# One kernel, four edits: logits in the last block, high parts gathered first, ring pieces returned singly, own buffers for the adaLN blocks

## The reference

```
mod = silu(c) @ ada_w + ada_b                    # 1024 x 6144: six vectors of 1024
u   = rms_norm(x) * (1 + scale_a) + shift_a
x   = x + gate_a * mixer(u)                      # w_in: 1024 x 10760, mLSTM and dilated attention,
                                                 # two branch projections, one output projection w_out
u   = rms_norm(x) * (1 + scale_f) + shift_f
x   = x + gate_f * moe(u)                        # 16 experts, top 2 of one group of 4
out = rms_norm(x) * final_norm_g

moe: scores = sigmoid(u @ router_w); two experts a row; weights = scores / their sum
     out += weight * ((silu(u @ w_gate[e]) * (u @ w_up[e])) @ w_down[e])   # 1024x512, 1024x512, 512x1024
```

## Time and profile before

| | |
|---|---|
| median of 3 runs | 637.62 us (637.15 to 639.16) |
| the profiled execution, its own time | 639.07 us |
| its span in the trace | 637.30 us |
| PE busy | 593.4 us, 93% |
| PE weight loads busy | 444.7 us, 70% |
| DVE, ACT busy | 326.7 us (51%), 225.2 us (35%) |
| read from HBM | 183.16 MB, 289 GB/s over the span |

### The profile page before, as it was taken

How to read it: one execution, slowest core, us unless ns; L and a number is a source line. 1 busy time by engine, 2 the same in 40 slices (tenths; PEclk the granted TensorE clock), 3 DMA queues, 4 the chain that set the end, 5 groups by cost and what they waited for, 6 DMA issues and landing times.

```text
span 637.3 us, 8441 instructions
## 1 busy us (share of the span) xinstructions
PE 593.4 (93%) x3581; PEld 444.7 (70%) x3581; DVE 326.7 (51%) x515; ACT 225.2 (35%) x300; POOL 5.6 (1%) x13
## 2 busy tenths in 40 slices
PE   4697999999999999999999999889999999998783
PEld 4697988999998888999999886533543533533231
DVE  3895986775758977787454655302212112120103
ACT  3424658544454365665552443201111111110103
POOL 3000000000000000000000000000000000000000
PEclk9997999999999999999999997799999999999997
DMA  8996454877767867725699699199999999999981
GB/s 314 358 359 229 143 194 133 283 259 242 255 216 264 319 214 261 258 77 195 198 338 344 219 374 388 48 398 387 401 387 402 386 401 387 401 387 401 387 325 67
DMA packets 86313, 184.78 MB, mean 290 GB/s; under 512 B 5401, under 2 KB 5505, under 8 KB 86273
## 3 DMA queue, kind: packets, MB, share of 16 engines
q1 hardware_dynamic: 83746, 184.06, 79.9%
q10 hardware_dynamic: 2528, 0.16, 0.3%
HBM read 183.16 MB, written 1.05 MB: 289 GB/s over the span
## 4 chain that ended last, share of the span: by engine, by line
PE 85%; DMA 8%; DVE 3%; ACT 1%; issue 1%; SPq 1%; DVEq 0%; ACTq 0%
PE ps L1287 32%; PE ps L1295 15%; PE ps L1495 14%; PE ps L1506 7%; DMA ring<-in_w_down_e_dram 3%; PE ps L1485 2%; DMA ring<-in_w_gate_e_dram 2%; DMA ring<-in_w_up_e_dram 2%; PE ps L1529 2%; DMA raw<-in_ada_w_dram 1%; PE ps L1235 1%; PE ps L1358 1%; PE ps L1382 1%; PE ps L1397 1%; PE ps L1244 1%
## 5 line engine op out<-in xcount | busy, mean ns | idle before, releaser
L1287 PE MATMUL ps<-u_hi,hi 128*128 128x256 f32 x448 | 130.8, 292 | 9.3 <-DVE u_lo L815 9.3
L755 DVE TENSOR_TENSOR lo<-raw,hi 128x2048 fp32r<-128x2048 f32 x52 | 118.7, 2289 | 35.6 <-ACT hi L514 35.3
L1287 PE MATMUL ps<-u_lo,hi 128*128 128x256 f32 x448 | 128.7, 287 | 0.0
L1287 PE MATMUL ps<-u_hi,lo 128*128 128x256 f32 x448 | 128.6, 287 | 0.0
L1495 PE MATMUL ps<-ring,xe_t 128*64 128x512 f32 x512 | 113.8, 594 | 7.9 <-DMA ring<-in_w_up_e_dram 4.4
L514 ACT CAST hi<-raw 128x2048 fp32r<-128x2048 f32 x52 | 98.8, 1907 | 50.0 <-PE ps L1287 24.8
L1287 PEld LDWEIGHTS ps<-u_hi,hi 128*128 128x128 f32 x448 | 88.0, 196 | 9.6 <-DVE u_lo L815 9.5
L1495 PEld LDWEIGHTS ps<-ring,xe_t 128*64 128x64 f32 x512 | 37.1, 137 | 76.0 <-issue 75.7
L1287 PEld LDWEIGHTS ps<-u_lo,hi 128*128 128x128 f32 x448 | 88.0, 197 | 0.1
L1287 PEld LDWEIGHTS ps<-u_hi,lo 128*128 128x128 f32 x448 | 87.9, 196 | 0.0
L1506 PE MATMUL ps<-ring,he_t 128*64 128x512 f32 x256 | 57.1, 596 | 1.5 <-DMA ring<-in_w_down_e_dram 0.8
(11 more groups left out here) (276 smaller groups left out, 797.0 us busy)
## 6 DMA issues: line engine op xcount, KB each, us to landing
raw<-in_w_in_dram SPq DMA_DIRECT2D x42, 1024.0 KB, 5.3
ring<-in_w_gate_e_dram SPq DMA_DIRECT2D x32, 1024.0 KB, 14.6
ring<-in_w_up_e_dram SPq DMA_DIRECT2D x32, 1024.0 KB, 14.2
ring<-in_w_down_e_dram SPq DMA_DIRECT2D x32, 1024.0 KB, 14.6
raw<-in_ada_w_dram SPq DMA_DIRECT2D x24, 1024.0 KB, 5.5
raw<-in_w_branch_m_dram SPq DMA_DIRECT2D x4, 1024.0 KB, 5.5
raw<-in_w_out_dram SPq DMA_DIRECT2D x4, 1024.0 KB, 7.5
raw<-in_w_branch_a_dram SPq DMA_DIRECT2D x2, 1024.0 KB, 6.4
```

Source lines behind the costliest of these rows:

```text
L755: V.tensor_tensor(lo[b % RING][:], src[:], hi[b % RING][:].bitcast(F32), ALU.subtract).then_inc(lo_ready, 1)
L1287: ins = mm(dst, w[:, k, cols], x[:, k0 + k, :], start=(first and c % 2 == 0 and k == 0 and n == 0), stop=(end and k == KB - 1 and n == 2), ...
```

## The change

1. **ada blocks.** The eight first ada blocks get buffers of their own (`first_ada`), so that the w blocks 0 to 3 and the ada blocks are all loaded without waits but two. A block is now 256 rows (two a partition) by shift and scale columns together, landed by two transfers of 512 KB. All eight are DVE's, two instructions of 128x(2x512) each. The sixteen later ones are one row a partition by 2048 columns, one DVE instruction each. ACT instead of DVE scales x; two matmuls on x are put ahead of its transposes; block 0 takes its contraction step by step, as quarters of u_lo come.
2. **Last block.** The first half of the logits goes between t=0 and t=1 of the last block, the transposes of x_res for t=0 into its t=1.
3. **Gather.** xg_lo is computed behind the one-hot tables, and the first gather takes all high parts and then all low parts.
4. **Pieces.** `chunk_used` counts pieces, not half groups; each piece is waited for and returned by itself. For that the four matmuls of one expert stand together. A ring slot moves from 120 to 176 KB, and so do xg_hi and result in exchange.

```diff
+        first_ada = [at(f"first_ada{a}", k, [P, 2, 2, NB]) for a, k in enumerate((96, 104, 112, 144, 48, 72, 164, 156))]
...
+            for kind, n in FIRST:
+                if kind == "w":
+                    sp.dma_start(raw[n][:], block_source((kind, n))).then_inc(raw_loaded[n], 16)
+                else:
+                    if n == 6:
+                        after(sp, "x_ss")
+                    if n == 7:
+                        after(sp, "x_t")
+                    j, k = n // KB, 2 * (n % KB)
+                    for i in range(2):
+                        sp.dma_start(first_ada[n][:, i], ada_first[:, k + i, 0:2, j * NB:(j + 1) * NB]
+                                     ).then_inc(ada_landed[n], 16)
...
-            ada(1)
+            for a in range(4):
+                ada(a)
+                if a == 0:
+                    after(dve, "vec_t")
+                    event(V.tensor_copy(vec[:], ps[0][:, 0:104]), "vec")
+            split_lo(0)
+            modulate(0, 1)
+            split_first()
+            split_lo(1)
             ada(4)
             ada(5)
-            modulate(0, 1)
-            split_lo(0)
-            u_split_lo(0)
-            split_lo(1)
-            ada(2)
-            ada(3)
...
+                    for c in range(4):
+                        if s == EARLY - 1 and c == 2:
+                            after(pe, "x_up")
+                            mod_columns(1, 7)
...
+                            if s == NBLK - 1 and t == 1 and k == 1:
+                                after(pe, "x1_1_t0")
+                                for c in range(KB):
+                                    tr_ins = tr(ps[6][:, c * P:(c + 1) * P], x_res[:, 0, NB + c * P:NB + (c + 1) * P], ident[:])
+                                event(tr_ins, "x1_turn1_t0")
                         if s == NBLK - 1 and t == 0:
                             event(ins, "wo_t0")
+                            after(pe, "x1_turned0", "mod3")
+                            logits(0, 0)
+                            logits(1, 0)
...
             def gate_or_up(bank, half, slots, col):
 
-                for k in range(KB):
-                    kk = KB * half + k
-                    for s in range(2):
-                        w = ring[slots[s]][:].rearrange("p (k n) -> p k n", k=KB)
+                for s, slot in enumerate(slots):
+                    w = ring[slot][:].rearrange("p (k n) -> p k n", k=KB)
+                    for k in range(KB):
+                        kk = KB * half + k
                         ins = mm(ps[bank][64 * s:64 * s + 64, :], xe_t[:, kk, col + s * SLOTS:col + (s + 1) * SLOTS], w[:, k, :],
                                  start=(kk == 0), stop=(kk == KT - 1))
-                ins.then_inc(group_used, 1)
+                    ins.then_inc(chunk_used, 1)
...
-            pe.wait_ge(xg_split, TT)
+            after(pe, "xg_hi1")
             pe.wait_ge(onehot_ready, 1)
             for kb in range(4):
-                gather_part(kb, 4 * SLOTS, 4 + kb)
+                gather_part(kb, 4 * SLOTS, 4 + kb, (0,))
+            pe.wait_ge(xg_split, TT)
+            for kb in range(4):
+                gather_part(kb, 4 * SLOTS, 4 + kb, (1,))
```

More of the change, by code:

```diff
@@ L528, in _ @@
             event(A_(st[:, 4:6], st[:, 2:4], ACT.Sqrt), "x_sqrt")
+            after(act, "x_rms")
+            for t in range(TT):
+                ins = A_(x_in[:, t, :], x_in[:, t, :], ACT.Copy, scale=st[:, 6 + t:7 + t])
+            event(ins, "x_norm")
             act.dma_start(w_if[:], A["w_in"][0].rearrange("(k p) n -> p k n", p=P)[:, :, IF_AT:IF_AT + IF_N]).then_inc(small_loaded, 16)
@@ L542, in u_split_hi @@
                 event(ins, f"u_hi{j}")
-            split_hi(0)
-            u_split_hi(0)
+            after(act, "x_up", "chan0")
+            for k in range(KB):
+                event(A_(u_hi[:, k, :], x_t[:, k, :], ACT.Identity, scale=chan[:, 2, k:k + 1], bias=chan[:, 0, k:k + 1]),
+                      f"u_hi0_{k}")
             split_hi(1)
@@ L758, in ada @@
             def ada(a):
+                if a < ADA_FIRST:
+                    j = a // KB
+                    dve.wait_ge(ada_landed[a], 32)
+                    dst = acc_a[:, :, j * NB:(j + 1) * NB]
+                    if a % KB:
+                        dve.wait_ge(ada_done, a)
+                    for i in range(2):
+                        kk = 2 * (a % KB) + i
+                        if kk == 0:
+                            step(V.tensor_scalar(dst, first_ada[a][:, i], cs[:, 0:1], None, ALU.mult))
+                            continue
+                        ins = V.scalar_tensor_tensor(out=dst, in0=first_ada[a][:, i], scalar=cs[:, kk:kk + 1], in1=dst,
+                                                     op0=ALU.mult, op1=ALU.add)
+                        if i == 0:
+                            step(ins)
+                    ins.then_inc(ada_done, 1)
+                    return
@@ L769, in ada @@
[L769 to L779 removed]
+                if k:
+                    dve.wait_ge(ada_done, a)
@@ L810, in modulate, with split_first @@
                 event(ins, f"u_f32_{j}")
+            def split_first():
+                after(dve, "u_f32_0")
+                for k in range(KB):
+                    after(dve, f"u_hi0_{k}")
+                    event(V.tensor_tensor(u_lo[:, k, :], u_f32[:, k, :], u_hi[:, k, :].bitcast(F32), ALU.subtract), f"u_lo0_{k}")
             def u_split_lo(j):
@@ L1100, in _ @@
                                       st[:, 28 + t:29 + t], None, ALU.mult)
-            for t in range(TT):
-                after(dve, f"xg_hi{t}")
-                V.scalar_tensor_tensor(out=xg_lo[:, t, :], in0=x_res[:, t, :], scalar=st[:, 14 + t:15 + t],
-                                       in1=xg_hi[:, t, :].bitcast(F32), op0=ALU.mult, op1=ALU.subtract).then_inc(xg_split, 1)
             after(dve, "rank_sums")
@@ L1156, in _ @@
             build_onehot(0)
+            for t in range(TT):
+                after(dve, f"xg_hi{t}")
+                V.scalar_tensor_tensor(out=xg_lo[:, t, :], in0=x_res[:, t, :], scalar=st[:, 14 + t:15 + t],
+                                       in1=xg_hi[:, t, :].bitcast(F32), op0=ALU.mult, op1=ALU.subtract).then_inc(xg_split, 1)
             event(V.tensor_scalar(many_i[:, 0:1], many[:, 0:1], float(SLOTS), None, ALU.is_gt), "many")
@@ L1256, in _, with logits @@
             event(ins, "x_t")
-            pe.wait_ge(rows_loaded, 80)
-            event(tr(ps[0][:, 0:104], rows[0:104, :], ident[0:104, 0:104]), "vec_t")
-            mod_columns(0, 0, 1)
-            mod_columns(0, 1, 1)
+            mod_columns(0, 1)
+            def logits(t, h):
+                for k in range(KB):
+                    ins = mm(ps[4][:, t * NE:(t + 1) * NE], x_res_t[h][:, k, t * P:(t + 1) * P], rw_scaled[:, KB * h + k, :],
+                             start=(t == 0 and h == 0 and k == 0), stop=(h == 1 and k == KB - 1), skip_group_check=True)
+                return ins
             for s, (g, k0, first, end) in enumerate(BLOCKS):
                 kind, _, channel_major = GROUP_LIST[g]
-                if s == 0:
-                    after(pe, "u_lo0", "x_up")
                 if s == EARLY:
```

232 lines of the change are left out of this document (107 added, 125 removed).

## The result

| | before | after |
|---|---|---|
| median | 638.39 us (637.15 to 639.40, 4 runs) | 655.65 us (654.55 to 656.03, 4 runs) |
| span of the profiled execution | 637.30 us | 653.70 us |
| PE busy | 593.4 us, 93% | 618.6 us, 95% |

The changed kernel is slower: ratio 1.0268, interval 1.0243 to 1.0294. The forecast was 651 us, in a range of 628 to 662.

The account below looks back on a forecast made before the run. In the expert stage PE and DMA are both full, PE only 8.7 us faster. Head -6.0, last block and gather -1.2, expert stage +20.5 make +13.3 us: 650.9 by the median of 637.62, called 651; range 628 to 662.

Parts of the forecast that it names:

- The order of the matmuls: Expert stage: one expert's four matmuls together start the second expert four passes late; +20.5 us net of 8.7 us of waits.
- the DMA share: Expert stage, sign in the profile after: the DMA share would be below 1 after 415 us.
- the estimate of five instructions waiting ahead of a column half: PE's queue in the expert stage: 28 instructions shared, then five before each column half; gives a lag of four passes.
- 17 runs x 1.72: Expert stage: each of 17 runs of half groups pays four passes, 1.72 us, once at its end; 29.2 us in all.
- The head: Start up to block 3, ada blocks and PE's earlier start, with the clock staying up: -6.0 us (1.4 to 9.4).
- The estimate of an ada instruction of 1024: Head, on DVE: one ada instruction of 1024 takes some 1.3 us, 2.6 a block (bounds 0.78 and 1.56).
- Last block and gather: Between the head and the expert stage: net -1.2 us for the stage's start (bounds -3.0 and +0.5).
- The block's share: Last block: logits and transposes moved in delay its end 2.4 us but save one turn; +0.8 us (+2.3 to -1.0).
- the gather's: Gather: xg_lo, 2.48 us, leaves the way of the rank sums; about 2.0 us gained.
- The single returns: Expert stage: returning one piece at a time gains nothing on the first release and nothing at the end.
- PE passing all sixteen instructions: Expert stage rival: the new order costs nothing, DMA stays the bound; -7.2 us, 630.4 us; chance 0.31 with short lags.
- lags of one or two: Expert stage: second expert starting one or two passes late, 7.3 us per pass on PE, would give 630 to 635 us.

Follow-up runs that it names:

- e1: Kernel before with only the loop order changed: one expert's four matmuls stand together ahead of the other's; 661.74 us, ratio 1.0368.
- e3: Changed kernel with the experts taking turns of two matmuls each; 630.80 us, ratio 0.9888.
- e4: Changed kernel with turns of three matmuls of the first expert, three of the second, then one and one; 636.59 us, ratio 0.9977.
- g3: e2 with all eight matmuls of the first expert ahead of the second's eight, in the first pair's gate only; 640.21 us in one run.
- f1: e2 with last block and gather as in the kernel before; 632.94 us, ratio 0.9917.
- e2: Changed kernel with only the turns restored, one matmul of each expert in turn; single waits and releases stay; 630.30 us, ratio 0.9880.
- f2: e2 with the last block alone as in the kernel before, logits behind it; 629.28 us, ratio 0.9864.
- g1: e2 with logits behind the last block (f2) and the last eight pieces loaded in halves (f4); 628.87 us, ratio 0.9857.
- f3: e2 with waits and returns by half group, two pieces at a time; 632.44 us, ratio 0.9898.
- f4: e2 with the last eight pieces each loaded as two transfers of 512 KB; 628.82 us, ratio 0.9856.

## Why the prediction was right

**The order of the matmuls decides: right.** Forecast: a lag of four passes, a gate group of some 8.8 us, no PE wait on ring pieces. Seen: 4 passes begun in the first 1.78 us and 8 in the next 1.72, 8.94 us, no wait. One sign did not come as forecast: the DMA share did not fall below 1 after 415 us but stayed at 1.04 up to 563, and fell only when the loads were all in. The slower PE did not hold the loads up; it fell behind them. e1 shows the cause by itself, 23.6 us; e3, e4 and g3 show the count behind it (0, 2 and 12 passes where the estimate of five instructions waiting ahead of a column half says 0, 2 and 12). The Trainium skill (TensorE: Matmul & The Clock Gate, Part 3, The mechanism) has matmuls in program order in start and end; here the second expert's first pass begins together with the first expert's fifth, at 401.88, and ahead of its last three, so that between the two column halves this does not hold. Its queue of 64 (the table at its start), whose window it gives for weight loads, does not cover it either: eight instructions, passes among them, can be passed without loss, sixteen cannot.

**Its size: some 4 us too small.** I took 17 runs x 1.72 = 29.2 us. A run of two costs 1.85 and a run of four 2.07, so 10 x 1.85 + 7 x 2.07 = 33.0: beside the four passes each change from one half group to the next costs another 0.1 us or so, which four passes of 0.43 leave out; what makes it up was not looked into. 33.0 - 8.7 = 24.3, against 23.35 + 0.4 measured.

**The head: right in sum and parts.** Forecast 6.0; the books give 6.1, f1 5.3 in the times and 5.6 in the trace. The first block at 27.25 (forecast 27.0), block 3's at 49.92 (49.7), the idle stretch ahead of it 1.05 us (about 1), and the clock of 54 to 85 us at 1.00 instead of 0.93. The estimate of an ada instruction of 1024, 1.3 us, held: DVE took 8.03 us for six of them, 1.34 each, and was through with the first four blocks at 20.65 (20.5).

```profile
12.62 8.03 DVE L797 SCALAR_TENSOR_TENSOR acc_a<-first_ada,cs,acc_a 128x1024 f32<-128x1024 f32 x6
```

**Last block and gather: right at the clock of the profiled run.** Forecast -1.2, measured -1.3 in the books, where both kernels ran the larger part of the gather at the lower clock. The block's share was +0.8 and came out as +1.0 by the traces of e2 and f2; the gather's was -2.0 and came out as -2.3 by what is left in the books, and as -2.6 at most between f1 and g1. What the prediction left out is that the clock there changes from run to run and moves the start of the experts by up to 2 us: the 3.7 us between f1 and f2 hold some of it. It held that at full clock 0.6 us of xg_lo would show; f2 ran the gather at full clock, and 0.15 us showed. That the profiled run fell where the working assumed it was luck.

**The single returns: right.** Costed at nothing, and f3 gives 0.1 us.

**The rivals.** PE passing all sixteen instructions would come to the same as turns restored: 7.2 us faster than before. Those measured 638.17 - 630.30 = 7.9 us (6.6 to 8.7 by the interval), so the sum without the order's cost held. That 630.3 stands so close to the forecast 630.4 is partly chance, since the forecast went by 637.62 us for the kernel before and e2 stands beside 638.17. The "630 to 635" for lags of one or two was a slip: by the prediction's own 7.3 us for each pass a lag of two gives 14.6 - 8.7 - 7.2 = -1.3, so 636.3 us, and e4, with that lag, measured 636.6.

**The total.** Forecast +13.3 us, measured +16.4 between the two profiled executions and +17.3 between the medians. Of the 3.1 us between the first two, the order's cost makes 3.3 (23.35 + 0.4 measured, 20.5 forecast), and the head and the middle gained 0.1 each more than forecast. The other 0.9 us lie between profiled executions and medians, and no term of the sum stands for them.

## What to carry to other kernels

Where small matmuls share the array by column halves, let them take turns in the program: here two of one expert in a row were free and four cost 1.85 us at every run of half groups. Before making an engine's order serve a finer hand-over, compare its cost with the slack of that engine (8.7 us here) and with what the finer hand-over can bring (0.1 us). Test such an order on its own: three edits that gained 8 us were hidden behind one that lost 25.

## What was not expected of the hardware

**The clock behind the last block is not the same from run to run.** Up to the first gather matmul the changed kernel, e2, e3, e4, f3 and f4 differ in nothing on PE. Granted clock in 384 to 391 us, when PE has just had gaps of 0.7 us between small matmuls: the changed kernel, at the lower level of 1.2 GHz, then e2, between the two levels.

```profile
384.00:391.00 7.00, 6.62 (x14) 3.89 (x15) 4.25 (x26) 4.07 (x6) 0.00 (x0) 0.51 0.90 346
```

```profile
384.00:391.00 7.00, 6.29 (x16) 2.94 (x17) 4.98 (x29) 4.18 (x6) 0.00 (x0) 0.76 0.94 360
```

The 16 matmuls on the high parts took 3.65 us in the changed kernel, 3.40 in e2 and 2.14 in f4, and the first gate matmul came at 400.15, 399.02 and 398.12. That is 2 us between executions of one program up to there, about as much as each of the small edits is worth.

**A matmul of one column half can begin ahead of earlier ones of the other, but only over a short reach.** While PE works through one expert's instructions, those of the other are reached once no more than about five are left ahead; the count held for lists of 8, 12, 16 and 32. Two short queues, one before each column half, behind a longer shared one are an estimate that gives these counts. No run tested the length of the shared one, and another build of the queue that gives the same counts is not ruled out.
